# Merging in token chunks, with the router's norm computed from sums taken in the merge

## The reference, cut to what matters

```python
def rmsnorm(x, g):
    y = x * lax.rsqrt(jnp.mean(x * x, axis=-1, keepdims=True) + EPS)
    return y * g
def merge_branches(branches, g_out, w_out):        # two branches of 512 channels
    y = jnp.concatenate([rmsnorm(br, g) for br, g in zip(branches, gains)], axis=-1)
    return y @ w_out
# x = x + gate * merge_branches(...);  h = rmsnorm(x, g) * (1 + scale) + shift;  x = x + gate2 * hier_moe(h)
```

## Time and profile before

| what | value |
|---|---|
| median of three runs | 2589.18 us |
| the profiled execution | 2590.3 us |
| its span | 2588.5 us |
| TensorE busy | 2243.1 us, 87% |
| VectorE (DVE) busy | 739.0 us, 29% |
| ScalarE (ACT) busy | 597.7 us, 23% |
| products of the merges (L1191) | 254.2 us, 640 instructions |
| evictions of the merges (L1230) | 27.9 us, 40 |
| mean granted TensorE clock | 0.918 |

### The profile page before, as it was taken

One profiled execution on the slowest core, in us unless ns is written; L12 is line 12 of the kernel. 1 busy time (PEld: TensorE's weight loads), 2 busy tenths in 40 slices (PEclk: granted clock), 3 DMA queues, 4 the chain that ended last, 5 costly groups with the idle time before them and its releaser, 6 DMA issues. The chain is left out here.

```text
span 2588.5 us, 34779 instructions
## 1 busy us (share of the span) xinstructions
PE 2243.1 (87%) x15176; PEld 1072.6 (41%) x15176; DVE 739.0 (29%) x1096; ACT 597.7 (23%) x908; POOL 180.6 (7%) x126
## 2 busy tenths in 40 slices
PE   4799998978995699999999739998995999998874
PEld 3577875534453333333333224443443333332222
DVE  3423226642005211111111183665215111110104
ACT  4421105540004111111111134664003111111111
POOL 0000000000000000000000021342000000000002
PEclk8799999979997799999999958999896999999986
DMA  8101107046631889889999450001004999999995
GB/s 328 38 25 33 41 16 317 1 125 223 236 130 52 320 357 418 353 347 415 418 413 417 148 171 17 25 25 59 15 3 162 419 414 408 416 426 412 427 426 210
DMA packets 139498, 595.82 MB, mean 230 GB/s; under 512 B 25332, under 2 KB 52688, under 8 KB 114640
## 3 DMA queue, kind: packets, MB, share of 16 engines
q1 hardware_dynamic: 109232, 515.42, 50.0%
q0 software_dynamic: 11952, 43.52, 4.6%
q10 hardware_dynamic: 18160, 34.61, 3.6%
HBM read 534.79 MB, written 58.72 MB: 229 GB/s over the span
## 5 line engine op out<-in xcount | busy, mean ns | idle before, releaser
L1615 PE MATMUL ph<-w,x_t 128*32 128x512 f32 x6016 | 687.2, 610 | 36.7 <-DMA w<-in_exp_w 34.3
L1615 PEld LDWEIGHTS ph<-w,x_t 128*32 128x32 f32 x6016 | 193.0, 112 | 453.6 <-issue 429.2
L1628 PE MATMUL py<-w,g_t 128*32 128x512 f32 x3008 | 341.1, 594 | 1.0 <-DVE g_t L1734 1.0
L1728 DVE TENSOR_TENSOR hidden<-hidden,ph 64x512 f32<-64x512 f32 x94 | 102.1, 1086 | 759.1 <-ACT hidden L1686 759.1
L1191 PE MATMUL z<-Y,w_o 128*128 128x512 f32 (+1 forms) x640 | 254.2, 555 | 0.0
L1686 ACT ACTIVATE hidden<-ph 64x512 f32<-64x512 f32 x94 | 55.5, 590 | 698.5 <-PE ph L1615 698.5
L1940 PE MATMUL z<-hT,w_cd 128*128 128x512 f32 (+1 forms) x448 | 184.1, 569 | 4.9 <-ACT hT L488 4.9
L1628 PEld LDWEIGHTS py<-w,g_t 128*32 128x32 f32 x3008 | 93.6, 110 | 205.1 <-issue 203.7
L702 PE MATMUL z<-h_high,w_hi 128*128 128x512 f32 (+1 forms) x432 | 161.7, 374 | 15.4 <-DVE h_low L536 15.4
L1593 POOL DMA_INDIRECT x_rows<-h_tokens,index x47 | 44.3, 943 | 1848.4 <-PE px L1600 982.2
L1191 PEld LDWEIGHTS z<-Y,w_o 128*128 128x128 f32 x640 | 120.9, 192 | 120.7 <-issue 116.7
(11 more groups left out here) (305 smaller groups left out, 2052.7 us busy)
## 6 DMA issues: line engine op xcount, KB each, us to landing
w<-in_exp_w SPq DMA_DIRECT2D x192, 2048.0 KB, 15.8
ada_raw<-in_ada_w SPq DMA_DIRECT2D x24, 2048.0 KB, 8.2
y_slots<-y_rows ACTq DMA_DIRECT2D x188, 128.0 KB, 9.1
y_slots<-zero SPq DMA_DIRECT2D x29, 512.0 KB, 14.7
h_tokens<-h_rows ACTq DMA_DIRECT2D x18, 512.0 KB, 2.9
w_ab<-in_w_in_ab SPq DMA_DIRECT2D x14, 512.0 KB, 3.8
w_cd<-in_w_in_cd SPq DMA_DIRECT2D x12, 512.0 KB, 3.8
x_t_saved<-xT SPq DMA_DIRECT2D x8, 640.0 KB, 8.9
```

Of the source, the lines that this page charges most:

```text
L1615: ins = pe.matmul(ph[row:row + UNIT, :], xt[:, k, at:at + UNIT], w13[place[2 * b + n] % RING][:, half, k, :], start=(k == 0), stop=(k == K ...
L1628: ins = pe.matmul(py[b % 2][row:row + UNIT, :], gt[:, k, n * UNIT:(n + 1) * UNIT], w2[place[2 * b + n] % RING][:, k, half * 512:(half + 1) ...
L1728: dve.tensor_tensor(hid[PAIR:P, :].rearrange("s (k q) -> s q k", k=FT), hid[0:PAIR, :].rearrange("s (q k) -> s q k", k=FT), ph[PAIR:P, :]. ...
```

## The change

`merge` works in chunks of tokens as the outer order: squares, sums, roots, spreads and scaling are done for each chunk (the spreads go into three separate PSUM tiles), and the products of all eight output tiles of a chunk come before those of the next. After the eviction of each product ACT squares the new x and DVE adds it up; TensorE makes the sums of a finished chunk between later products, and the last chunk's after the last. Variance, root and reciprocal go into a small tensor `rstd` that lives through the program, and `route` takes it: its norm starts with the spread. The output matrix is requested with a semaphore for each half, and in layer 0 an ada unit is requested behind each half. The folds of ada units 0 and 1 move behind the first product.

```diff
...
+            self.rstd = self.sb(top, "rstd", [P, NT])
...
+        if not n["given"]:
+            for k in range(KT):
+                act.activation(hT[:, k, 0:tok], self.xT[:, k, 0:tok], ACT.Square).then_inc(n["sq"], 1)
+            act.wait_ge(n["var"], 1)
+            act.activation(n["rows"][:, 1, 0:n["nt"]], n["rows"][:, 0, 0:n["nt"]], ACT.Sqrt).then_inc(n["std"], 1)
...
     def norm_pe(self, pe, n, hT, ps_sum, ps_bc):
-        pe.wait_ge(n["acc"], KT - 1)
+        if not n["given"]:
+            pe.wait_ge(n["acc"], KT - 1)
+            for t in range(n["nt"]):
+                ins = pe.matmul(ps_sum[:, t:t + 1], hT[:, 0, t * P:(t + 1) * P], self.c("ones", 1), start=True, stop=True)
+            ins.then_inc(n["sum"], 1)
+            pe.wait_ge(n["rstd"], 1)
         for t in range(n["nt"]):
-            ins = pe.matmul(ps_sum[:, t:t + 1], hT[:, 0, t * P:(t + 1) * P], self.c("ones", 1), start=True, stop=True)
-        ins.then_inc(n["sum"], 1)
-        pe.wait_ge(n["rstd"], 1)
-        for t in range(n["nt"]):
-            ins = pe.transpose(ps_bc[:, t * P:(t + 1) * P],
-                               n["rows"][:, 3, t:t + 1].to_broadcast([P, P]), self.c("ident"))
+            of = self.rstd[:, t:t + 1] if n["given"] else n["rows"][:, 3, t:t + 1]
+            ins = pe.transpose(ps_bc[:, t * P:(t + 1) * P], of.to_broadcast([P, P]), self.c("ident"))
         ins.then_inc(n["bc"], 1)
...
     def merge(self, layer, nt):
...
+        UNITS = KT * NC
+        own = [slice(at, at + size) for at, size in chunks]
+        tiles = [range(at // P, (at + size) // P) for at, size in chunks]
+        rows_of = [slice(t[0], t[-1] + 1) for t in tiles]
...
+            x_rows = self.sb(ctx, "x_stat_rows", [P, 2, NT])
+            x_acc = self.sb(ctx, "x_squares", [P, tok])
+            x_sq = self.sb(ctx, "x_square", [P, 2, 512])
+            bc = [self.ps(ctx, f"bc{i}", [P, 512]) for i in range(3)]
...
+            def added(n):
+                return n - n // KT if n >= 0 else 0
 
             @block.sync
             def _(sp):
-                if ada:
-                    for h in range(HERE):
-                        self.ada_load(sp, ada, h)
                 for k in range(2):
                     cols = slice(k * 512, (k + 1) * 512)
                     if layer == 0:
                         for g in range(NKV):
                             sp.dma_start(w[g * HD:(g + 1) * HD, 0:BR, cols],
                                          self.i["w_out"][layer, g * (ATT_W // 2):(g + 1) * (ATT_W // 2), cols]
-                                         .rearrange("(k d) n -> d k n", d=HD)).then_inc(s_w, 16)
+                                         .rearrange("(k d) n -> d k n", d=HD)).then_inc(s_w[k], 16)
                         rest = BR
                     else:
                         rest = 0
                     sp.dma_start(w[:, rest:, cols],
-                                 self.i["w_out"][layer, rest * P:, cols].rearrange("(k p) n -> p k n", p=P)).then_inc(s_w, 16)
+                                 self.i["w_out"][layer, rest * P:, cols].rearrange("(k p) n -> p k n", p=P)).then_inc(s_w[k], 16)
+                    if ada:
+                        self.ada_load(sp, ada, k)
                 if ada:
...
+                def squares(c, ks):
+                    for k in ks:
+                        act.activation(sq[:, k, own[c]], self.Y[:, k, own[c]], ACT.Square).then_inc(s_sq, 1)
+
+                def roots(c):
+                    act.wait_ge(s_var, c + 1)
+                    act.activation(rows[:, 1, :, rows_of[c]], rows[:, 0, :, rows_of[c]], ACT.Sqrt).then_inc(s_std, 1)
+
+                def x_roots(c):
+                    act.wait_ge(s_var, NC + c + 1)
+                    act.activation(x_rows[:, 1, rows_of[c]], x_rows[:, 0, rows_of[c]], ACT.Sqrt).then_inc(s_std, 1)
+
+                squares(0, range(2 * BR))
+                squares(1, range(BR))
+                roots(0)
+                if ada:
+                    self.ada_row_out(act, ada, 0)
+                squares(1, range(BR, 2 * BR))
+                if NC > 2:
+                    squares(2, range(2 * BR))
+                roots(1)
                 if ada:
                     self.ada_row_out(act, ada, 1)
-                for br in range(2):
-                    act.wait_ge(s_var, br + 1)
-                    act.activation(rows[:, 1, br, 0:nt], rows[:, 0, br, 0:nt], ACT.Sqrt).then_inc(s_std, 1)
-                if ada:
-                    for h in range(HERE, NA):
-                        self.ada_row_out(act, ada, h)
+                for n in range(UNITS):
+                    c, m = divmod(n, KT)
+                    act.wait_ge(s_x, n + 1)
+                    if m == 0:
+                        act.activation(x_acc[:, own[c]], self.xT[:, m, own[c]], ACT.Square).then_inc(s_xq, 1)
+                    else:
+                        if added(n - 2):
+                            act.wait_ge(s_xa, added(n - 2))
+                        act.activation(x_sq[:, n % 2, 0:chunks[c][1]], self.xT[:, m, own[c]], ACT.Square).then_inc(s_xq, 1)
+                    if n == 1 and NC > 2:
+                        roots(2)
+                    if HERE <= n + 1 < NA:
+                        self.ada_row_out(act, ada, n + 1)
+                    if c and m == 3:
+                        x_roots(c - 1)
+                x_roots(NC - 1)
...
+                def sums(c):
+                    pe.wait_ge(s_acc, 2 * (BR - 1) * (c + 1))
+                    if c:
+                        pe.wait_ge(s_var, c)
+                    for br in range(2):
+                        for t in tiles[c]:
+                            ins = pe.matmul(branch_sums[:, br, t:t + 1], sq[:, br * BR, t * P:(t + 1) * P], self.c("ones", 1),
+                                            start=True, stop=True)
                     ins.then_inc(s_sum, 1)
+
+                def x_stats(c):
+                    pe.wait_ge(s_xa, added(c * KT + KT - 1))
+                    pe.wait_ge(s_var, NC + c)
+                    for t in tiles[c]:
+                        ins = pe.matmul(x_sums[:, t:t + 1], x_acc[:, t * P:(t + 1) * P], self.c("ones", 1), start=True, stop=True)
+                    ins.then_inc(s_sum, 1)
+
+                def spread(c):
+                    pe.wait_ge(s_r, c + 1)
+                    for br in range(2):
+                        j = 2 * c + br
+                        if j >= 3:
+                            pe.wait_ge(s_n, BR * (j - 2))
+                        for i, t in enumerate(tiles[c]):
+                            ins = pe.transpose(bc[j % 3][:, i * P:(i + 1) * P], rows[:, 2, br, t:t + 1].to_broadcast([P, P]),
+                                               self.c("ident"))
+                        ins.then_inc(s_bc, 1)
+
+                sums(0)
                 if ada:
+                    self.ada_pe(pe, ada, 0)
+                spread(0)
+                sums(1)
+                if ada:
+                    self.ada_pe(pe, ada, 1)
+                for n in range(UNITS):
+                    c, m = divmod(n, KT)
+                    at, size = chunks[c]
+                    if c == 0 and m in (0, KT // 2):
+                        pe.wait_ge(s_w[2 * m // KT], 48 if layer == 0 else 16)
                     if n >= 2:
                         pe.wait_ge(s_x, n - 1)
                     for k in range(2 * BR):
+                        if m == 0:
+                            pe.wait_ge(s_n, 2 * BR * c + k + 1)
                         ins = pe.matmul(z[n % 2][:, 0:size], w[:, k, m * P:(m + 1) * P], self.Y[:, k, at:at + size],
                                         start=(k == 0), stop=(k == 2 * BR - 1))
                     ins.then_inc(s_z, 1)
+                    if n == 0:
+                        if ada:
+                            for h in range(HERE):
+                                self.ada_turn(pe, ada, h)
+                        spread(1)
+                        if NC > 2:
+                            sums(2)
+                    if n == 2 and NC > 2:
+                        spread(2)
+                    if HERE <= n + 1 < NA:
                         self.ada_pe(pe, ada, n + 1)
+                    if HERE <= n < NA:
                         if n == HERE:
                             pe.wait_ge(ada["read"], 1)
                         self.ada_turn(pe, ada, n)
+                    if c and m == 1:
+                        x_stats(c - 1)
+                x_stats(NC - 1)
...
+                def adds(c, br):
+                    total = sq[:, br * BR, own[c]]
+                    for k in range(1, BR):
+                        done = 2 * (BR - 1) * c + (BR - 1) * br + k
+                        dve.wait_ge(s_sq, 2 * BR * c + br * BR + k + 1)
+                        dve.tensor_tensor(total, total, sq[:, br * BR + k, own[c]], ALU.add).then_inc(s_acc, 1)
+                        dve.wait_ge(s_acc, done)
+
+                def variances(c):
```

(92 more changed lines are left out.)

81 lines of the change are left out of this document (25 added, 56 removed).

## The result

The changed kernel takes 2561.66 us (median of four runs, 2559.63 to 2565.53) against 2589.19 for the kernel before, measured alongside it (four runs, 2586.84 to 2597.45): ratio 0.9889, 95% interval 0.987 to 0.9907. The profiled execution went from 2590.3 to 2562.43 us. So 27.9 us are gone in the profiled execution where the prediction had summed 30.6.

What follows compares the result with a forecast made beforehand. Stages run one behind another, with merge bodies bound by TensorE and the router's norm all path. From 2590.3 us, 33.6 − 1.5 − 5.2 + 3.3 + 0.4 = 30.6 gave 2559.7, median 2558.6; range 2550 to 2568.

Steps and rivals of the forecast that it cites:

- router, block start to logits: Both layers' routers: removing the norm gains 33.6 us, late input DMAs cost 1.5.
- tails, last eviction to block start: Ends of both merges: added adds, sums and roots cost 5.2 us, 3.4 in layer 1 and 1.8 in layer 0.
- head and body of layer 1: Layer 1's merge: first eviction at +25.4 instead of +30.9 gains 5.5 us, narrow groups cost 2.2; net 3.3.
- head and body of layer 0: Layer 0's merge: earlier second unit gains 3.1 us, spread and x sums in the body cost 2.7; net 0.4.
- Router's norm: First ACT instruction to spread in the router disappears: 18.4 us in layer 0, 15.2 in layer 1, gain 33.6.
- The term of the late inputs: Logits wait for five small router DMAs: cost 0.3 us in layer 0, 1.2 in layer 1, 1.5 together.
- Layer 0's queue: Layer 0's merge requests: ada unit 0 lands near 570.3, the second matrix half near 578, unit 1 near 583.7.
- the second unit starts at 598.3: Layer 0's merge: second unit starts when TensorE finishes folds, spread and sums; first unit now ends at 601.4, gain 3.1 us.
- The marks: Signs: layer 0's merge 233 to 238 us, layer 1's near 135, logits 5.8 to 6.2 in, products 6.87 apart.
- The body: Rest of the merges: ACT's added 0.53 us square and DVE's 0.79 add fit in each 6.87 us unit, cost 0.

Runs made afterwards that it cites:

- e9: The changed kernel profiled again, unaltered, as a third look at the clock; single time 2560.08 us.
- e4: Kernel before, old order and requests, plus squares and sums of new x in the merge, router's norm starting with the spread: 2560.35 us, ratio 0.9879.
- e6: Changed kernel with the router's weights on their own semaphore, so the logits wait only for these: 2558.57 us, ratio 0.9879.
- e1: Changed kernel with both ada units requested ahead of the output matrix, as before the change: 2551.66 us, ratio 0.9839.
- e5: Changed kernel with each unit's square and add done three times, extra results unused: 2565.05 us, ratio 0.9908.
- e3: Changed kernel without squares, adds and sums of the new x; the router makes its norm itself: 2584.06 us, ratio 0.998.
- e7: Changed kernel with ada and half-matrix requests alternating, heads reordered, narrow groups apart and router weights on their own semaphore: 2545.41 us, ratio 0.9827.
- e2: Changed kernel with chunk 1's spread and chunk 2's sums and spread moved behind later products: 2559.23 us, ratio 0.9883.
- e8: The changed kernel profiled once more, unaltered, to look at the clock in layer 0's second product; single time 2559.07 us.

## Why the prediction was right, and where it was not

The gain by the prediction's own terms, in us (measured: stretches between the marks named above, in the profiled execution and in e9, the execution of the same kernel whose clock stayed up):

| term | forecast | profiled | e9 |
|---|---|---|---|
| router, block start to logits (norm removed, inputs late) | 33.6 − 1.5 = 32.1 | 18.43 + 14.67 = 33.1 | 33.3 |
| tails, last eviction to block start | −5.2 | −1.56 − 3.37 = −4.9 | −4.9 |
| head and body of layer 1 | 3.3 | 4.88 − 1.76 = 3.1 | 3.0 |
| head and body of layer 0 | 0.4 | 3.94 − 7.21 = −3.3 | 0.2 |
| sum | 30.6 | 28.0 | 31.5 |

- **Router's norm: right.** It is the gain: e4, which does this alone and pays the tails for it, saves 26.15. The reason it could be read off beforehand is that it was all path. The term of the late inputs was mis-sized: I took the fifth request at 3 us into layer 1's block, it stands at 2.1 (1926.15 against 1924.02), so the logits came 0.57 late instead of 1.2, and in layer 0 not at all. In the kernel before, one of the four requests ahead of the fifth took 1.72 us (layer 0) or 1.33 (layer 1) to issue; in the changed one none takes over 0.6. Why is open. e6 shows what there was to win.
- **Tails: right**, 1.6 and 3.4 for 1.8 and 3.4. The chained add of 512 columns cost 0.74 (1.48/2), estimated 0.79.
- **Layer 1: right** within 0.2. The first eviction came at +26.0 for +25.4, since the clock rose 5.1 us into the product and not 3.8 (the slice at 1810 has 0.85). The two narrow groups in the body cost 1.76 for 2.2.
- **Layer 0's queue: right.** Ada unit 0 landed at 570.95 (forecast 570.3) and unit 1 at 585.09 (583.7), and the first product came at 588.50 (587.4). The rates of 199 and 391 GB/s carried it: the window at 571 shows 205. The Trainium skill ("SBUF — State Buffer", section "Door 1: The DMA port swizzle (why [64,N] ≈ [32,N])") gives about 218 GB/s for a transfer to partitions 0 to 63; the 199 and 205 lie 6 to 9% below that. Added up again, the prediction's own terms (start at 556.3, 8.0 for a half, 5.4 for a unit) give 569.7 and 583.1, some 0.6 less than it wrote, so the landings were 1.3 and 2.0 late by them. What the prediction did not do is ask what the old order would have given. e1 answers: 10 us. The prediction priced the requests as the change has them, and so summed a loss into the term without seeing it.
- **The failed step: "the second unit starts at 598.3", and from there on units at 6.87.** It started at 599.19, and then took 10.18 us. The prediction had TensorE's clock only rise once dense work had warmed it; it never asked what the 3.7 us of folds, spread and sums would do to it, though it had put them there itself (2 × 1.05, 1.1 and 0.5; the 0.5 was too low by itself, since these sums are eight instructions and take 0.95 at full clock). That is 10.18 − 7.11 = 3.1 us, and 0.3 more in the sums (1.26 for 0.95). e9, where it did not happen, has 0.2 in this row for the forecast 0.4.
- **The marks.** The merge of layer 0 lasts 238.5 us between blocks (793.32 − 554.82; 233 to 238 foreseen, and 235.0 in e9) and that of layer 1 135.2 (near 135). Units are 6.87 apart and the expert stages are unchanged. The logits came 5.85 us into the block in layer 0, but 5.27 in layer 1, where 5.8 to 6.2 was foreseen for both: the mis-sized input term again.
- **The body: right.** Squares and adds cost nothing, even threefold (e5).

So the kernel's gain has two values. In an execution where the clock stays up it is 31.5, one more than forecast; where it falls, 28.0. The forecast of 2558.6 lies 3.1 below the median of 2561.66. That much is the clock's size, but three of its four runs carry no trace, and how many of them fell stays open.

**What the parts are worth.** Chunk order alone gave 5.8 (e3), the sums alone 26.15 (e4), and both 31.5 in e9 and 28.0 where the clock fell. They add up to within 0.5. The chunk order with its requests is thus a small part, which lost most of its worth to the order of the DMAs and sometimes 3 us to the clock. With both mended, and e6's 0.6 us with them, it is worth 412.8 − 364.4 − 26.2 = 22 us in the sections (e7).

**What stays open:** what sets the moment at which the clock rises, with which the later fall went in all seven executions, and whether that moment is the cause or only goes with it. The 3.5 us in e2 can't be credited to its edit: one execution without a fall shows the same, and its clock had risen early (0.36). e7 gives one more without a fall; neither shows that spreading the narrow work prevents it.

## What to carry to other kernels

Look for a statistic that a stage computes behind a barrier while every other engine is idle, and take its parts in the stage before, behind each tile as it is produced: with 6.12 us of idle time per unit on DVE, an added 0.7 us there and 0.6 on ACT were free, and only the last tile's share showed. When work is put ahead of a first product, list the requests on its queue in the order in which they are needed: two ada units that the first product waits for, one requested behind half of a matrix and one behind the whole, cost 10 us here. And narrow matmuls collected in one gap between wide ones are a risk to the clock (3 of 7 executions); spreading them over several gaps cost nothing in e2, but that it helps is not shown.

## What the hardware did that I had not expected

TensorE's granted clock fell from 1.00 to 0.50 (2.4 to 1.2 GHz) while TensorE was busy all the time, in a stretch of 3.7 us of matmuls of 1, 2 and 128 columns, and stood there for six microseconds of 512-column matmuls before it rose again. The same program did it in two of three profiled executions and not in the third, and over seven executions the fall went with a difference of under 0.1 us in when the clock had risen. Behind narrow groups of 1 to 2 us between products it was seen in no execution here. The Trainium skill ("TensorE: Matmul & The Clock Gate", "Part 4: PE-mode transpose") says that transposes don't count as busy in the way other matmuls do; the fall here agrees with that, but the stretch also holds folds and sums that are no transposes, and no run here took the spread alone away from it. The same page ("Part 1: The HAM clock gate (the "warmup" mystery)", under "What's actually happening") says of the rise that it differs from run to run; e8 and e9 show the like for the fall.

The narrow sums did not bring it up either. In layer 1 the product at 1805.20 follows 3.6 us of one-column sums, and the clock rose only 5.1 us into it. The price of a one-column sum was 0.22 us at 0.50 and 0.12 to 0.13 at 1.00, so where it stands counts as much as how many there are.
